# Odd layer of a two-layer trunk: eight row-tile steps of the attention set behind the projection tiles

## What is computed

```python
def heads(p):                                    # p = u @ w_in
    qw, kw, vw, qn, kn, vn = jnp.split(p, splits, axis=-1)
    qw = rms_norm(qw.reshape(b, l, WIN_Q_HEADS, HEAD_DIM), q_norm_win)   # 8 heads of 64
    kw = rms_norm(kw.reshape(b, l, WIN_KV_HEADS, HEAD_DIM), k_norm_win)  # 2 heads
    qn, kn = ...                                 # 8 heads each, normalised too
qwc, kwc, vwc, qnc, knc, vnc = heads(uc @ w_in)  # context
qwl, kwl, vwl, qnl, knl, vnl = heads(ul @ w_in)  # latent
qwl = apply_axial_rope(qwl, cos, sin); kwl = apply_axial_rope(kwl, cos, sin)
# window attention: softmax over [local scores (masked), context scores, a sink]
# neighbourhood attention: softmax over [local scores + relative bias, context scores]
ol = jnp.concatenate([window_attention(...), neighbourhood_attention(...)], axis=-1) @ w_out
```

## Time and profile before

| what | us |
|---|---|
| median of 3 runs | 1227.27 |
| lowest, highest | 1227.12, 1229.33 |
| the profiled execution | 1227.61 |
| its span | 1225.8 |
| PE busy in the span | 1165.4 (95%) |
| DVE busy in the span | 854.1 (70%) |
| ACT busy in the span | 600.9 (49%) |

### The profile page before, as it was taken

One profiled execution on the slowest core, in us unless ns is written; L12 is line 12 of the kernel. 1 busy time (PEld: TensorE's weight loads), 2 busy tenths in 40 slices (PEclk: granted clock), 3 DMA queues, 4 the chain that ended last, 5 costly groups with the idle time before them and its releaser, 6 DMA issues.

```text
span 1225.8 us, 17195 instructions
## 1 busy us (share of the span) xinstructions
PE 1165.4 (95%) x6430; PEld 933.3 (76%) x6430; DVE 854.1 (70%) x1254; ACT 600.9 (49%) x1048; POOL 87.2 (7%) x73
## 2 busy tenths in 40 slices
PE   5999899998987999999999999999899899999998
PEld 3567676776766788887887887887688569898997
DVE  5573797897967566896684684797676986755655
ACT  5430464737557335831331421446745777744543
POOL 0000102010020015000000000034000004000000
PEclk9999999999999999999999999999899999999999
DMA  9856343331421224454544543542334004555554
GB/s 361 347 214 247 103 130 95 98 120 45 142 78 61 87 88 147 170 187 149 191 155 137 205 138 135 206 154 69 103 121 137 19 1 138 168 185 189 182 187 155
DMA packets 49893, 179.13 MB, mean 146 GB/s; under 512 B 5216, under 2 KB 7584, under 8 KB 47776
## 3 DMA queue, kind: packets, MB, share of 16 engines
q1 hardware_dynamic: 49536, 177.66, 42.1%
q10 hardware_dynamic: 288, 0.56, 0.1%
HBM read 177.05 MB, written 1.15 MB: 145 GB/s over the span
## 4 chain that ended last, share of the span: by engine, by line
PE 72%; DVE 16%; ACT 6%; issue 3%; DMA 2%; DVEq 0%; SPq 0%; ACTq 0%
PE ps L1887 46%; PE ps L1894 9%; PE ps L2181 7%; DVE cacc L1585 4%; PE ps L1979 2%; ACT ey L1233 1%; DVE sm L1835 1%; DMA mhalf<-in_w_mod 1%; PE ps L1910 1%; DVE ey L1661 1%; DVE mixF L1687 1%; DVE xbc L1598 1%; DVE prob L1860 1%; DVE ycomb L1672 1%; DVE cacc L1582 1%
## 5 line engine op out<-in xcount | busy, mean ns | idle before, releaser
L1379 DVE TENSOR_TENSOR w_lo<-raw,w_hi 128x1024 fp32r<-128x1024 f32 x206 | 262.9, 1276 | 89.1 <-ACT w_hi L1018 88.9
L1018 ACT ACTIVATE w_hi<-raw 128x1024 fp32r<-128x1024 f32 x206 | 216.8, 1053 | 195.3 <-DMA raw<-in_w_ff 155.8
L1887 PE MATMUL ps<-a_hi,w_hi 128*128 128x512 f32 (+1 forms) x820 | 299.7, 365 | 0.0
L1887 PE MATMUL ps<-a_hi,w_lo 128*128 128x512 f32 (+1 forms) x820 | 289.4, 353 | 0.0
L1887 PE MATMUL ps<-a_lo,w_hi 128*128 128x512 f32 (+1 forms) x820 | 289.2, 353 | 0.0
L1887 PEld LDWEIGHTS ps<-a_hi,w_hi 128*128 128x128 f32 x820 | 155.7, 190 | 25.1 <-issue 2.8
L1887 PEld LDWEIGHTS ps<-a_lo,w_hi 128*128 128x128 f32 x820 | 155.7, 190 | 23.3 <-issue 1.0
L1887 PEld LDWEIGHTS ps<-a_hi,w_lo 128*128 128x128 f32 x820 | 155.6, 190 | 21.4
L1887 PE MATMUL ps<-b_hi,w_hi 128*128 128x512 f32 x304 | 119.2, 392 | 0.0
L1887 PE MATMUL ps<-b_lo,w_hi 128*128 128x512 f32 x304 | 118.5, 390 | 0.0
L1887 PE MATMUL ps<-b_hi,w_lo 128*128 128x512 f32 x304 | 118.3, 389 | 0.0
(11 more groups left out here) (288 smaller groups left out, 1762.8 us busy)
## 6 DMA issues: line engine op xcount, KB each, us to landing
raw<-in_w_ff SPq DMA_DIRECT2D x128, 512.0 KB, 3.5
mring<-in_w_mod SPq DMA_DIRECT2D x32, 768.0 KB, 5.2
raw<-in_w_in_even SPq DMA_DIRECT2D x36, 512.0 KB, 5.8
mring<-in_w_mod SPq DMA_DIRECT2D x16, 1024.0 KB, 6.9
ey<-acum_rows SPq DMA_DIRECT2D x32, 384.0 KB, 4.8
raw<-in_w_in_odd SPq DMA_DIRECT2D x18, 512.0 KB, 3.5
mhalf<-in_w_mod SPq DMA_DIRECT2D x16, 512.0 KB, 9.5
raw<-in_w_out_even SPq DMA_DIRECT2D x16, 512.0 KB, 3.5
```

The costliest lines, as they stand in the source:

```text
L1018: nc.scalar.activation(w_hi[:, u % RING, :, :], raw[:, u % RING, :, :], ACT.Copy).then_inc(hi_done, 1)
L1379: v.tensor_tensor(w_lo[:, u % RING, :, :], raw[:, u % RING, :, :], w_hi[:, u % RING, :, :].bitcast(F32), ALU.subtract).then_inc(lo_done, 1)
L1887: ins = mm(out_ap, w_[:, n % RING, k, :], (x_[k][:, 0:ntok] if type(x_) is list else x_[:, k, 0:ntok]), start=(k == 0 and j == 0), stop=(k ...
```

## The change

The order of the projection tiles becomes `v.0 kw.0 kn.0 kn.1 qw.0 qw.1 kn.2 qw.2 qw.3 kn.3 v.1 qn.0 v.2 qn.1 v.3 qn.2 v.4 qn.3`. From slot 9 on every slot ends with one call of `attend(n - 10)`. Up to j = 7, which stands in slot 17 behind the last projection tile, `attend(j)` emits `S` j+1, `scale` j, `PT` j, `max` j+1, `O` j-1, `exp` j+1, and for even j from 2 on `ohi` and `olo`. From j = 8 on it emits the order of before, with scores two steps ahead. Waits become waits by tile: `S` for the rotation or the normalisation of its own query tile, `O` for its own value tile. The scores up to step 8 use the bank pair 4, 5 alone, since the products still need banks 0 and 1; `hstat` of `kn.3` and of all `qn` uses bank 7, since `PT` uses bank 3. The results of the first four head tiles go to buffers of their own (`o_hi`, `o_lo`), since `a_hi` and `a_lo` are still read by the projections; `prob` and `pT` get other places.

```diff
-       for kind, i in (q.split(".") for q in ("v.0 kw.0 kn.0 kn.1 qw.0 qw.1 v.1 qw.2 qw.3 v.2 qn.0 qn.1 kn.2 qn.2 qn.3 kn.3 v.3 v.4").split())]
+       for kind, i in (q.split(".") for q in ("v.0 kw.0 kn.0 kn.1 qw.0 qw.1 kn.2 qw.2 qw.3 kn.3 v.1 qn.0 v.2 qn.1 v.3 qn.2 v.4 qn.3").split())]
+FIRST_STEP, BESIDE = 10, 8
...
-    for n in range(len(ODD) + 3):
-        if n == len(ODD) - 1:
-            s.append(("S", 0))
+
+    def attend(j):
+
+        if j == BESIDE:
+            s.append(("S", j + 1))
+        if j < BESIDE:
+            order = [("S", j + 1), ("scale", j), ("PT", j), ("max", j + 1), ("O", j - 1), ("exp", j + 1)]
+            if j >= 2 and j % 2 == 0:
+                order += [("ohi", j // 2 - 1), ("olo", j // 2 - 1)]
+        else:
+            order = [("S", j + 2), ("ohi", (j - 2) // 2), ("max", j + 1), ("scale", j), ("olo", (j - 2) // 2), ("exp", j + 1), ("PT", j), ("O", j - 1)]
+        for kind, i in order:
+            if kind in ("ohi", "olo"):
+                if j < BESIDE or j % 2 == 1:
+                    s.append((kind, i))
+            elif 0 <= i < len(ATTN):
+                s.append((kind, i))
+    for n in range(FIRST_STEP + len(ATTN) + 1):
         if n < len(ODD):
             gemm(*ODD[n][:2])
-        if n == len(ODD) - 1:
-            s.append(("max", 0))
...
-    n = len(ATTN)
-    for j in range(-1, n + 1):
-        for kind, i in (("S", j + 2), ("ohi", j - 2), ("max", j + 1), ("scale", j), ("olo", j - 2), ("exp", j + 1), ("PT", j), ("O", j - 1)):
...
+        if n >= FIRST_STEP - 1:
+            attend(n - FIRST_STEP)
...
-            job(st, B_AUX[n_aux % 2], freed=("hv_done", nk))
+            job(st, B_AUX[n_aux % 2 if st[1:] != ("kn", 3) and st[1] != "qn" else 1], freed=("hv_done", nk))
...
-                job(st + (par,), (B_SEG, B_GEMM[0])[st[1] % 2] + par)
+                job(st + (par,), (B_SEG, B_GEMM[0])[st[1] % 2 if st[1] > BESIDE else 0] + par)
...
-            job(("Opair", t), (B_Y, B_AUX[1])[t % 2], freed=("split_done", 5 * KT + t + 1), filled=("pv_done", 4 * t + 4))
+            job(("Opair", t), B_AUX[1] if t >= 4 and t % 2 == 0 else B_Y, freed=("split_done", 5 * KT + t + 1), filled=("pv_done", 4 * t + 4))
...
+        attn_hi = [o_hi[:, k, :] if k < 4 else a_hi[:, k, 0:SEQ] for k in range(KT)]
+        attn_lo = [o_lo[:, k, :] if k < 4 else a_lo[:, k, 0:SEQ] for k in range(KT)]
...
-                        pe.wait_ge(rope_done, len(rot_n))
-                    if t == 4:
-                        pe.wait_ge(qn_done, len(hn_n))
+                    if qt == 0 and t < 4:
+                        pe.wait_ge(rope_done, rot_n[("rot", "qw", t)] + 1)
+                    if qt == 0 and t >= 4:
+                        pe.wait_ge(qn_done, hn_n[("hnorm", "qn", t - 4)] + 1)
...
-                    if i == 0:
-                        pe.wait_ge(vtok_done, 5)
+                    if qt == 0:
+                        pe.wait_ge(vtok_done, 1 if t < 4 else t - 2)
```

More of the change, by code:

```diff
@@ L299, in script @@
         s.extend(("dup",) for o in behind(4) if o[0] == "kw")
-    n = len(ATTN)
-    for j in range(-1, n + 1):
-        for kind, i in (("S", j + 2), ("ohi", j - 2), ("max", j + 1), ("scale", j), ("olo", j - 2), ("exp", j + 1), ("PT", j), ("O", j - 1)):
[L303 to L308, removed]
+        if n >= FIRST_STEP - 1:
+            attend(n - FIRST_STEP)
+    s += [("ohi", len(ATTN) // 2 - 1), ("olo", len(ATTN) // 2 - 1)]
     s += [("grow",), ("vprep", NORM_FF1)]
@@ L613, in trunk @@
         vtok = place("vtok", [P, NCH, 5 * P])
+        vtok_end = at[0]
         at[0] = max(at[0], region + 2 * 16384)
@@ L621, in trunk @@
         bias = place("bias", [P, 2, 8, SEQ], offset=region + 16384)
-        prob = place("prob", [P, 3, 2, T], offset=region + 32768)
-        pT = place("pT", [P, 2, 2, T], offset=region + 32768 + 12288)
+        prob = place("prob", [P, 3, 2, T], offset=macc_at + 7680)
+        pT = place("pT", [P, 2, 2, T], offset=vtok_end)
+        assert vtok_end + 8 * 2 * T <= region + 16384
+        o_hi = place("o_hi", [P, 4, SEQ], F32R, offset=hr_at)
+        o_lo = place("o_lo", [P, 4, SEQ], F32R, offset=hr_at + 4 * 4 * SEQ)
         fin = place("fin", [P, 2, D], offset=out_at)
@@ L725, in operands @@
                 return mix_hi[half], mix_lo[half]
+            if st[1] == "outO":
+                return attn_hi, attn_lo
             return a_hi, a_lo
@@ L1367, in _ @@
                     act.wait_ge(*filled(("Opair", st[1])))
-                    nc.scalar.activation(a_hi[:, st[1], 0:SEQ], ps[:, b, 0:SEQ], ACT.Copy).then_inc(signal(ohi_done), 1)
+                    nc.scalar.activation(attn_hi[st[1]], ps[:, b, 0:SEQ], ACT.Copy).then_inc(signal(ohi_done), 1)
         @block.vector
@@ L1864, in _ @@
                     b, _ = jobs[("Opair", t)]
-                    v.tensor_tensor(a_lo[:, t, 0:SEQ], ps[:, b, 0:SEQ], a_hi[:, t, 0:SEQ].bitcast(F32), ALU.subtract).then_inc(signal(split_done), 1)
+                    v.tensor_tensor(attn_lo[t], ps[:, b, 0:SEQ], attn_hi[t].bitcast(F32), ALU.subtract).then_inc(signal(split_done), 1)
                 elif k == "out":
```

## The result

The changed kernel takes 1248.37 us (median; 1247.78 to 1249.76), the kernel before 1227.33: the ratio is 1.0169, 95% interval 1.0152 to 1.0187. It is slower by 21 us. The forecast was 1242.0, 14.7 us slower. The result lies in the stated range, 1233 to 1249, but outside the forecast's own range, 1238 to 1245.

What follows compares the result with a forecast made beforehand. PE, busy 95% of the span, was taken as the bound. `max` 10 starting 12.7 us later plus 2.0 us of halved clock gave 14.7 us, 1242.0 us median; own range 1238 to 1245, stated range 1233 to 1249.

Steps and rivals of the forecast that it cites:

- the clock's rival: PE's clock falls at every stall: four more falls of 1 to 2 us each, 1246 to 1250 us; chance 0.13.
- PE is the bound, and the change can win only its idle time: Whole kernel: PE busy for 95% of the span; its odd-layer waits offer 7.1 us to win.
- 3.1 for no stalls at all: Slots 10 to 17, rival: PE fills its gaps and all stalls go, saving 3.1 us, 1224 us; chance 0.09.
- The ring: Slots beside attention steps: ACT, DVE and PE wait in a circle, 9.08 us against PE's 6.40 in `qn` slots.
- the waits of the pairs: Value slot plus `qn` slot, slots 12 to 17: PE waits 2.68 us in each of three pairs, 8.04 us.
- The other half of a pair has no wait: Value slots, 512 columns: the chain needs 7.08 us, PE's own work 9.00 us, so PE does not wait.
- Buffers, banks, waits by tile at nothing: Whole change: other buffers of the same shapes cost nothing; otherwise the attention's tail would leave 3.25 to 3.6 us a step.
- the forecast's sign: Expected evidence: tail steps of 3.25 to 3.6 us; 890.61 to `max` 10 some 110 us, 95.2 before.
- The clock: Behind the 5.5 us stall in slot 11: one fall to half clock, slowing `PT` 1 and `O` 0, 2.0 us.
- the long wait: Slot 11: PE waits 5.5 us before `PT` 1, for DVE's normalisation of `kn.3`, rotation of `qw.3` and scaling.
- The way out: Behind the projections: from `PT` 7 at 989.8 to `max` 10 at 998.5, 12.7 us later than before.
- The milder rival's sum: Pairs cost 1 us each and the long stall drops no clock: 14.7 - 2.0 - 5 to 7, 1233 to 1238; chance 0.12.

Runs made afterwards that it cites:

- e11_best: e6_all with result pairs' high part before the weights', rotations of slots 10 and 11 behind the scaling, slot 11's before its normalisation: 1227.9 us.
- e6_all: Changed kernel with the edits of e2_norm and e5_high_split together: 1230.05 us, ratio 1.0014.
- e2_norm: Changed kernel with each slot's normalisation, from slot 11 on, behind the attention step's scaling instead of ahead of it: 1235.4 us.
- e3_high: Changed kernel with only ACT's high part of the weight tile moved in front of the step's copies and exponentials: 1239.1 us.
- e5_high_split: Changed kernel with ACT's high part of the weight tile in front of the step and the result pair's split behind the next scaling: 1234.0 us.
- e7_behind: Changed kernel with all attention steps behind the last projection, in the order and with the two score pairs of before: 1231.0 us.
- e1_warm: Changed kernel with unused matmuls in front of the transposes of steps 1 (six), 3, 5, 7 and 8 (two each): 1242.5 us.
- e9_four: Changed kernel with four attention steps beside the projections instead of eight, from slot 14 on: 1236.6 us.
- e13_last: e11_best with one unused matmul of 512 columns in front of the transposes of step 8: 1228.9 us, ratio 1.0001.

## Why the prediction was right, and where it was off

The direction and the mechanism are right: stalls that come out of the order of the queues, of the forecast's size and in its places. The size is right only by the wide range. The forecast's own sum ended at 1245, and the result lies where the clock's rival had it, to which the forecast gave 0.13.

- *PE is the bound, and the change can win only its idle time.* Right, and it bounds the whole idea. The interleaving with most of its stalls gone (e11_best) makes the way 0.3 us shorter, where the forecast's sum gave 3.1 for no stalls at all. The longer products took some 1.2 us in e6_all; that waits in slot 10 and in the tail take the rest is argued and not tested.
- *The ring.* Right term by term: 9.03 us from `max` to the transposes forecast, 8.90 measured; waits of 2.68 forecast, 2.45 measured; 1.5, 0.75 and 5.5 forecast, 1.35, 1.05 and 5.51 measured. DVE waits in it for ACT's parts and ACT for DVE's `max`, as forecast. e2_norm, e3_high and e5_high_split take a leg of it away each, and the waits of the pairs and of slot 11 come within 0.2 us of what the sum says.
- *The other half of a pair has no wait.* Right: in the value slots PE's transposes follow the scores without a gap (scores at 945.68, transposes at 946.74).
- *Buffers, banks, waits by tile at nothing.* Right within 3 us by e7_behind. The tail's starts of `max` from 1006.11 to 1022.50 are 3.28 us apart on the average, in the 3.25 to 3.6 of the forecast's sign.
- *The clock.* This is the term that was mis-sized. I counted one fall, 2.0 us, and put the fall at every stall among the rivals with 0.13. The clock fell behind each of the three waits of 2.45 us and the one of 2.09 too. By e1_warm all falls together cost 6.1 us, 1.4 of them behind the long wait and 4.7 behind the others. The forecast had 2.0 for all of them, 4.1 too little; of the 5.8 us by which the way is longer than forecast that is the larger part, and the rest is not the clock.
- *The reason given against the falls.* It was that the trace has no case between 1.3 and 4.72 us. That holds for the odd layer alone. In the same trace PE waited 4.24 us at 386.00, and the clock fell behind it (the window below); 1.84 us at 25.85 and 0.71 at 27.20, and the granted clock is 0.50 from 28 to 30 us; and 1.63 and 1.64 us at 221.27 and 295.41, behind which it stayed at 1.00. So there was a fall behind a wait shorter than 2.68 us, and the rival deserved more than 0.13.

```profile
25.85 0.64 PE L1910 MATMUL ps<-mhalf,sil 128*32 128x256 f32 x8 [1.84 <-DMA mhalf<-in_w_mod]
```
```profile
386.00:388.00 2.00, 2.00 (x8) 1.70 (x9) 1.65 (x2) 2.00 (x7) 0.00 (x0) 0.58 0.04 8
```

- *The rule named beside that rival.* The Trainium skill ("TensorE: Matmul & The Clock Gate", Part 1: The HAM clock gate) has throttled as the default and activity as what releases it. By that rule the changed kernel's windows agree, 0.57 to 0.69 behind the waits and 1.00 again once PE had worked. The rule as the forecast gave it does not tell which waits are long enough.
- *The way out.* 8.7 us forecast from `PT` 7 to `max` 10, 10.45 measured; the row at 995.66 is still at full pace and the pieces after it are not. In e1_warm, which keeps the clock up, it is 8.86 (991.56 to 1000.42), so 1.6 of the 1.75 us are the clock. The way from 890.5 to `max` 10 is 115.6 us, where the forecast's sign had some 110, and 95.2 before.
- *The milder rival's sum.* 14.7 - 2.0 - 5 to 7 is 5.7 to 7.7, which gives 1233 to 1235 and not to 1238. It changes neither the forecast nor the range.

Still open: what the remaining 0.24% of e7_behind is made of, why a product behind an `O` or a score pair takes 0.2 us more, and what decides whether the clock falls behind a given short wait.

## What to carry to other kernels

In a kernel whose order is one list for all engines, a step set beside another couples every engine's queue: before it is moved, add up the ring (what the engines do one behind the other between two waits of the bounding engine) and compare it with that engine's own work in the same slot. Here 9.1 us stood against 6.4, and one move of 1.9 us of DVE's work behind the instruction that TensorE waits for gave 13 us back. Stalls of TensorE of some 2 us are to be priced with the halved clock behind them, here about 1.5 us each where TensorE sets the pace, though not every one of them had a fall behind it (2.29 us in e9_four). And where the bounding engine was idle for only 7 us before, an interleaving without its stalls may still win nothing, as in e11_best, whose ratio is 0.9998.

## What the runs showed of the hardware that I had not expected

- The clock fell behind single waits of 2.45, 2.26, 2.09 and 1.93 us, but not behind one of 2.29 us in e9_four (granted clock 1.00 from 978.8 to 982). Of three waits of 1.83 or 1.84 us in one run of e3_high one was followed by a fall (0.55 from 972.0 to 975.5) and two were not. In e11_best the clock fell behind 0.77 and 1.05 us with a score pair between; in e6_all the same pair of waits had no fall behind it. The length of the wait just before does not decide it. The Trainium skill ("TensorE: Matmul & The Clock Gate", Part 1: The HAM clock gate) calls the window in which activity is counted free-running, which fits equal waits with different sequels; the runs here cannot show it.
- The fall can come after the wait: behind the one that ends at 975.77 the transposes still take 1.13 us, and only the next piece takes 1.98. Behind the one that ends at 936.12 the transposes themselves take 1.97.
- Unused matmuls that take no more than the wait kept the clock at 1.00, and were worth 6 us where TensorE sets the pace (e1_warm) and nothing where DVE does (e13_last).
